# A decoder trunk on one core: four groups of modulation matmuls move to other places of the mixer, and two gate operations move behind a score update

## The chip, the cores and the metric

The kernel runs on one core of a Trainium2 chip. The metric is device time in microseconds (us), the median of three runs. The kernel before takes 1442.78 us (1442.36 to 1449.56). A profiled execution is taken beside the timed runs, and all durations below are from that one execution.

The core has a matrix engine (TensorE; PE in the rows, PEld for its weight loads), VectorE (DVE), ScalarE (ACT), GpSimd (POOL) and a queue engine (SP) that in this kernel issues the weight loads. Each engine works through its own list of instructions in order and waits on semaphores for the others.

## The reference

One step of a two-layer decoder trunk, for a prompt of 256 tokens and 8 single-token samples (264 columns together), with a model width of 1024, all in float32. A layer is: a SwiGLU block, a mixer, and a second SwiGLU block. Cut to what matters here:

```python
mod = (c @ w_ada[l] + b_ada[l]).reshape(B, N_SUB, 3, D_MODEL)   # adaLN: 9 blocks of 1024 columns a layer
h = ada_norm(x, norm_gain[l, 1], mod[:, 1, 0], mod[:, 1, 1])
y, ... = mixer_block(h, ...)          # branches A (HGRN2), B (RG-LRU), C (GLA), merged, times w_out
x = x + mod[:, 1, 2] * y

# branch B inside mixer_block
r, i = sigmoid(conv @ wa + ba), sigmoid(conv @ wx + bx)
log_a = -RG_C * r * softplus(-lam)
a, u  = exp(log_a), sqrt(-expm1(2 * log_a)) * i * conv
h_t   = a_t * h_(t-1) + u_t           # a scan over the tokens
y_b   = gelu(gb) * h
```

Branches A and C are gated linear recurrences. Inside a block of tokens the kernel forms their decayed scores in nine levels (pairs of tokens at distance 1, 2, 4, ... 128): at each level TensorE multiplies q and k, VectorE puts the result in the score tile and multiplies q, k and the decays for the next level.

## The kernel before

**Units.** The weights come as tiles of at most 128 x 1024 values (512 KB), called units here. Both layers have 436 units, 82 of them in each mixer. For a unit, SP loads a tile into one of six raw buffers; ScalarE rounds it to a high part (`whi`, line 450); VectorE subtracts to get the low part (`wlo`, line 458); and TensorE makes three matmuls for each 128 x 128 block (lines 493 to 495: high weight by high and by low activation, low weight by high activation), 24 in a full unit.

**Steps.** Every engine runs over the same list `MIX` of the mixer's 82 units, written out by hand. At step u, ScalarE and VectorE split unit u + 3 (`LOOK` is 3), then take the bank of unit u from TensorE, and then do whatever tables of numbers put at this step: `AT`, `EARLY_AT`, `HEAD_AT`, `PE_LV` for the score levels, `RG_AT` for branch B. The tables fix each engine's order at the time of writing; nothing is chosen at run time. In step u = `PE_LV` + 1, VectorE calls `keep` and `update` for a score level, and only after that come the entries of `RG_AT`. Unit numbers that matter below: 20 to 25 are branch B's gate weights and its `bg` columns, 26 to 29 are the values of branch C (`cv`), 30 to 33 and 34 to 37 the output gates of C (`cg`) and A (`ag`), and 38 to 45 the merge gate `ma`.

**The adaLN blocks.** `w_ada` is also read in tiles of 512 KB. Blocks 6 and 7 of a layer (the shift and scale of the second SwiGLU block) are computed inside the mixer, each in two groups of four tiles. The table `MIX_ADA` holds the units after which TensorE runs a group (line 679, 32 recorded matmuls); two steps after the second group of a block, VectorE turns the sums and adds the bias (lines 1730 and 1736), and after block 7 it also forms the norm's gains (line 1754).

**The raw buffers.** A group's four tiles use the same six raw buffers as the units. `load_order` puts them behind the load of unit place + 3. A load waits until the load six places earlier in the list has been used:

```python
            if c >= RAW:
                was, m = LOADS[c - RAW]
                if was == "m":
                    sp.wait_ge(lo_done, m + 1 + SLOTS)   # the unit's low part is made
                else:
                    sp.wait_ge(S["ada_used"], m + 1)     # TensorE has used the adaLN tile
```

So a group's last tile waits for the low part of unit place + 1, the next unit's load (place + 4) for that of place + 2, and the loads from place + 6 on for the group itself. SP issues in order, so a load that waits holds all behind it.

**Branch A's outer products.** At step 16 VectorE turns the samples' values (`vrA`); GpSimd writes them to memory (`v_rows`, line 1147) and reads them back spread over all partitions (`xA`, line 1161); ScalarE multiplies them at step 21.

**Branch B's gate.** `RG_AT` puts the two operations called `scaled` (lines 2207 and 2209: (r + 1) times the input, and the decay plus 1) at step 30, and the product `u` and the first half of the scan at step 32.

Of the kernel before, what the change touches and what calls it, by code (L numbers as in the profile page):

```python
# [48 lines left out]
    return l * UNITS + BASE[stage] + k  # L49


MIX_ADA = (10, 16, 29, 71)
ADA_BLOCKS = [(0, 1), (0, 0)]
ADA_FIRST = {}
RING = 8
# [3 lines left out]
def plan_ada():  # L59

    for l in range(NL):
        for f, places, blocks in (
                (0, (("in0", 16), ("in0", 28), ("in0", 41), ("out0", 11)), [(l, 2), (l, 3), (l, 4), (l, 5)]),
                (1, (("in1", 18), ("in1", 36), ("out1", 11)), [(l, 8), (l + 1, 0), (l + 1, 1)])):
            if f:
                for n, place in enumerate(MIX_ADA):
                    ADA_FIRST[(l, "mix", place)] = (8 * len(ADA_BLOCKS) + 4 * n, 4)
# [170 lines left out]


PE_LV = {'A': (17, 20, 24, 28, 31, 33, 38, 43, 45), 'C': (24, 28, 33, 38, 43, 45, 47, 50, 54)}  # L240
RG_AT = {'tanh': 22, 'gate': 25, 'exp': 26, 'square': 28, 'scaled': 30, 'root': 29, 'u': 32, 'scan': 32, 'y': 35, 'high': 37, 'low': 37}


BATCHES = [("A", 0), ("A", 1), ("A", 2), ("A", 3), ("C", 0), ("C", 1)]
# [2 lines left out]
def trunk(nc, x_prompt, x_sample, c_prompt, c_sample, state_hgrn, state_conv, state_rglru, state_gla,  # L247
# [4 lines left out]
    with ctx:  # L252
# [150 lines left out]
        def wait(eng, name, L, i=0):  # L403

            eng.wait_ge(S[name], L * PER[name] + i + 1)
# [95 lines left out]
        def evacuated(eng, L, what, j):  # L501

            group_done(eng, L, "mix", GI[(what, j)])
# [718 lines left out]
        def _(act):  # L1222
            def a(out, in_, func, **k):
                return nc.scalar.activation(out, in_, func, **k)  # L1224
# [28 lines left out]
            def A_(ins):  # L1253

                ins.then_inc(act_seq, 1)
                seq[0] += 1

            def own(L):
                act.wait_ge(act_seq, seq[0])
# [164 lines left out]
            def mixer(L):  # L1424
# [11 lines left out]
                for u, (kind, what, j) in enumerate(MIX):  # L1436
# [100 lines left out]
                    for t in range(2):  # L1537
                        if u == AT["C_vT"][t] + 1:
                            wait(act, "C_vT", L, t)
                            a(VT["C"][:, t], AUX[1][:, :], ACT.Copy).then_inc(S["C_vTe"], 1)  # L1540
                    if u == RG_AT["tanh"]:
                        evacuated(act, L, "wa", 3)
                        for jj in range(4):
                            c, c2_ = PC["nsp"] + jj, PC["nsp2"] + jj
                            A_(a(GT["A"][:, jj], tmp[:, 4 + jj], ACT.Tanh, scale=par_all[:, L, c:c + 1], bias=par_all[:, L, c:c + 1]))
                    if u == RG_AT["exp"]:
                        own(L)
# [4 lines left out]
                        last.then_inc(S["rg_tanh"], 1)  # L1552
                    if u == RG_AT["root"]:
                        wait(act, "rg_nt", L)
                        a(GT["A"][:, :], GT["A"][:, :], ACT.Sqrt).then_inc(S["rg_sqrt"], 1)
                    if u == RG_AT["high"]:
                        wait(act, "yb", L)
# [91 lines left out]
        def _(dve):  # L1649
# [12 lines left out]
            def V_(ins):  # L1662

                ins.then_inc(dve_seq, 1)
                seq[0] += 1
# [266 lines left out]
            def mixer(L):  # L1932
# [32 lines left out]
                def update(br, li):  # L1965

                    n_h = 4 if br == "A" else 2
                    q_, k_ = Q[br][:, :, 0:T], K[br][:, :, 0:T]
                    wait(dve, br + "_mm", L, li - 1)
                    if li == 1:  # L1970
                        if br == "A":
                            wait(dve, "A_f", L)
                        else:
                            wait(dve, "C_f", L)
                        tt(q_, q_, B[br][:, :, 0:T], ALU.mult).then_inc(S[br + "_up"], 1)
                        return
                    m = 2 ** (li - 2)
                    d = decay(br, m).rearrange("p h (n two o) -> p h n two o", two=2, o=1)
                    shape = [P, n_h, T // (2 * m), m]
                    qv, kv = halves(q_, m), halves(k_, m)  # L1980
                    if li < 9:
                        tt(qv[:, :, :, 1], qv[:, :, :, 1], bc(d[:, :, :, 0], shape), ALU.mult)
                    last = tt(kv[:, :, :, 0], kv[:, :, :, 0], bc(d[:, :, :, 1], shape), ALU.mult)
                    if li < 9:
                        dv = decay(br, m).rearrange("p h (n two) -> p h n two", two=2)
                        last = tt(decay(br, 2 * m), dv[:, :, :, 0], dv[:, :, :, 1], ALU.mult)
                    last.then_inc(S[br + "_up"], 1)
# [52 lines left out]
                for u, (kind, what, j) in enumerate(MIX):  # L2040
# [151 lines left out]
                    for br in "AC":  # L2192
                        for li in range(9):
                            if u == PE_LV[br][li] + 1:
                                keep(br, li)
                                update(br, li + 1)
                    if u == RG_AT["gate"]:
                        evacuated(dve, L, "wx", 3)
                        V_(v.scalar_tensor_tensor(bx, bx, 1.0, cv, ALU.add, ALU.mult))
                    if u == RG_AT["square"]:  # L2200
                        wait(dve, "rg_tanh", L)
# [141 lines left out]
```

## Time and profile before

| what | value |
|---|---|
| median of three runs | 1442.78 us |
| the profiled execution's own time | 1443.82 us |
| its span, first to last instruction | 1442.0 us |
| TensorE busy | 1421.0 us (99%) |
| VectorE busy | 940.0 us (65%) |
| ScalarE busy | 807.0 us (56%) |
| mean granted TensorE clock | 0.996 of full |
| DMA, mean over the span | 224 GB/s |

The table is read from the top: where one engine is busy nearly all the time, the others count only where they make it wait. The records of matmuls overlap (one lasts about 0.28 us, and the next starts 0.12 us after it), so short waits of TensorE have to be read from the distance of starts as well as from idle time. A mixer lasts some 287 us: the first from 246 to 533 us, the second from 948 to 1235 us.

### The profile page before, as it was taken

To read this page: it belongs to the slowest core of one execution; us is meant where nothing else is said; L and a number is where in the kernel's file an instruction comes from. 1 tells how busy PE (TensorE), PEld (TensorE's weight loads), DVE (VectorE), ACT (ScalarE), POOL (GpSimd) and SP (SyncE) were. 2 spreads that over 40 slices of the span, in tenths; PEclk is the share of its full clock that TensorE was granted. 3 is DMA by queue.
4 is the path that set the end of the run, shared out by engine and by line. 5 is a ranking of instruction groups with operands and counts; after the bars stand their busy time and mean duration, and the time that the engine had idled before them with its cause. 6 is when DMAs were issued, how large, how long until landed. Compare 5 with 4: busy or idle time off the path is not lost.

```text
span 1442.0 us, 32781 instructions
## 1 busy us (share of the span) xinstructions
PE 1421.0 (99%) x13780; PEld 1360.8 (94%) x13780; DVE 940.0 (65%) x1605; ACT 807.0 (56%) x1332; POOL 87.5 (6%) x131
## 2 busy tenths in 40 slices
PE   6999999999999999999999999999999999999998
PEld 4999999999999999999999999999999999999998
DVE  3665447788875697555586555577797677955553
ACT  2554435887666475444464434468876655644443
POOL 1040000001110120000000000000111002000000
PEclk9999999999999999999999999999999999999999
DMA  9988896698995679787768988776999657775661
GB/s 339 282 259 265 246 290 188 172 263 251 249 236 143 180 197 284 213 251 248 203 199 263 284 271 253 199 204 189 264 246 260 184 154 210 231 236 155 179 189 51
DMA packets 460036, 323.73 MB, mean 224 GB/s; under 512 B 11219, under 2 KB 435707, under 8 KB 459890
## 3 DMA queue, kind: packets, MB, share of 16 engines
q1 hardware_dynamic: 452240, 299.96, 71.1%
q0 software_dynamic: 6880, 20.41, 5.1%
q8 instruction: 109, 1.79, 0.5%
q10 hardware_dynamic: 770, 1.27, 0.2%
q14 instruction: 37, 0.30, 0.1%
HBM read 313.29 MB, written 8.37 MB: 223 GB/s over the span
## 4 chain that ended last, share of the span: by engine, by line
PE 88%; DVE 4%; issue 2%; ACT 2%; DMA 2%; SPq 1%; POOL 0%; DVEq 0%; ACTq 0%; POOLq 0%
PE bank L493 27%; PE bank L494 26%; PE bank L495 26%; PE bank L679 4%; SPq L551 1%; DVE wlo L458 1%; DMA first<-in_w_ada 1%; PE bank L846 1%; PE bank L874 1%; PE bank L893 1%; ACT whi L450 0%; ACT xA L1224 0%; DMA xA<-v_rows 0%; DMA v_rows<-vrA 0%; DVE x L1848 0%
## 5 line engine op out<-in xcount | busy, mean ns | idle before, releaser
L458 DVE TENSOR_TENSOR wlo<-raw,whi 128x1024 fp32r<-128x1024 f32 (+1 forms) x436 | 518.1, 1203 | 339.3 <-ACT whi L450 338.6
L493 PE MATMUL bank<-hH,whi 128*128 128x264 f32 x2048 | 587.1, 287 | 0.4 <-DVE wlo L458 0.4
L494 PE MATMUL bank<-hL,whi 128*128 128x264 f32 x2048 | 580.5, 283 | 0.0
L495 PE MATMUL bank<-hH,wlo 128*128 128x264 f32 x2048 | 580.0, 283 | 0.0
L450 ACT ACTIVATE whi<-raw 128x1024 fp32r<-128x1024 f32 (+1 forms) x436 | 442.2, 1033 | 185.6 <-PE bank L495 174.4
L493 PEld LDWEIGHTS bank<-hH,whi 128*128 128x128 f32 x2048 | 385.6, 188 | 13.9 <-issue 12.2
L494 PEld LDWEIGHTS bank<-hL,whi 128*128 128x128 f32 x2048 | 386.0, 188 | 0.0
L495 PEld LDWEIGHTS bank<-hH,wlo 128*128 128x128 f32 x2048 | 384.1, 188 | 0.0
L493 PE MATMUL bank<-hidH,whi 128*128 128x264 f32 x704 | 200.6, 285 | 0.0
L495 PE MATMUL bank<-hidH,wlo 128*128 128x264 f32 x704 | 200.1, 284 | 0.0
L494 PE MATMUL bank<-hidL,whi 128*128 128x264 f32 x704 | 199.5, 283 | 0.0
L1224 ACT ACTIVATE hidH<-hid 128x264 fp32r<-128x264 f32 x88 | 37.3, 424 | 173.0 <-DVE hid L1651 173.0
L493 PEld LDWEIGHTS bank<-hidH,whi 128*128 128x128 f32 x704 | 132.4, 188 | 1.3 <-issue 1.2
L495 PEld LDWEIGHTS bank<-hidH,wlo 128*128 128x128 f32 x704 | 132.7, 188 | 0.0
L494 PEld LDWEIGHTS bank<-hidL,whi 128*128 128x128 f32 x704 | 132.3, 188 | 0.0
L493 PE MATMUL bank<-uH,whi 128*128 128x274 f32 x320 | 94.5, 295 | 0.2
L494 PE MATMUL bank<-uL,whi 128*128 128x274 f32 x320 | 92.8, 290 | 0.0
L495 PE MATMUL bank<-uH,wlo 128*128 128x274 f32 x320 | 92.5, 289 | 0.0
L1224 ACT ACTIVATE sil<-bank 128x264 f32<-128x264 f32 x76 | 29.7, 391 | 98.5 <-PE bank L495 98.5
L493 PE MATMUL bank<-yH,whi 128*128 128x264 f32 x256 | 73.8, 288 | 0.0
L495 PE MATMUL bank<-yH,wlo 128*128 128x264 f32 x256 | 72.7, 284 | 0.0
L494 PE MATMUL bank<-yL,whi 128*128 128x264 f32 x256 | 72.6, 284 | 0.0
(330 smaller groups left out, 1659.1 us busy)
## 6 DMA issues: line engine op xcount, KB each, us to landing
raw<-in_w_ffn_in SPq DMA_DIRECT2D x176, 512.0 KB, 4.8
raw<-in_w_in SPq DMA_DIRECT2D x120, 512.0 KB, 5.6
ring<-in_w_ada SPq DMA_DIRECT2D x96, 512.0 KB, 6.6
raw<-in_w_ffn_out SPq DMA_DIRECT2D x64, 512.0 KB, 4.9
raw<-in_w_ada SPq DMA_DIRECT2D x32, 512.0 KB, 4.1
raw<-in_w_ffn_out SPq DMA_DIRECT2D x32, 384.0 KB, 4.7
first<-in_w_ada SPq DMA_DIRECT2D x16, 512.0 KB, 12.3
raw<-in_w_out SPq DMA_DIRECT2D x16, 512.0 KB, 5.3
```

Source lines behind the costliest of these rows:

```text
L450: nc.scalar.activation(whi[:, s, 0:w], raw[:, r, 0:w], ACT.Copy).then_inc(hi_done, 1)
L458: nc.vector.tensor_tensor(wlo[:, s, 0:w], raw[:, r, 0:w], whi[:, s, 0:w].bitcast(F), ALU.subtract).then_inc(lo_done, 1)
L493: nc.tensor.matmul(out, a, rh, start=start, stop=False)
L494: nc.tensor.matmul(out, a, rl, start=False, stop=False)
L495: return nc.tensor.matmul(out, b, rh, start=False, stop=stop)
L551: sp.dma_start(first[:, n], src).then_inc(first_in[FIRST_OF[n]], 16)
L679: last = mm(ps[32 * j:32 * j + 32, 0:256].rearrange("p (b i) -> p b i", i=32), cst[:, kt], src[:, j], start=(kt == 0), stop=(kt == KT - 1))
L846: last = mm(out, k_[:, r_], q_c, start=True, stop=True)
L874: mm(o, v0, sc[br][:, h, 0:T], start=True, stop=False)
L893: last = mm(AUX[base][0:dk, h * P:(h + 1) * P], KTT[br][:, t, h * dk:(h + 1) * dk], VT[br][:, t, h * P:(h + 1) * P], start=(t == 0), stop= ...
L1224: return nc.scalar.activation(out, in_, func, **k)
```

## The change

The groups stand after units 14, 28, 52 and 67 in place of 10, 16, 29 and 71, and `scaled` stands at step 32 in place of 30. No instruction is added or removed; both layers change alike.

```diff
-MIX_ADA = (10, 16, 29, 71)
+MIX_ADA = (14, 28, 52, 67)
-RG_AT = {'tanh': 22, 'gate': 25, 'exp': 26, 'square': 28, 'scaled': 30, 'root': 29, 'u': 32, 'scan': 32, 'y': 35, 'high': 37, 'low': 37}
+RG_AT = {'tanh': 22, 'gate': 25, 'exp': 26, 'square': 28, 'scaled': 32, 'root': 29, 'u': 32, 'scan': 32, 'y': 35, 'high': 37, 'low': 37}
```

The table moves instructions on TensorE, VectorE and SP; ScalarE and GpSimd keep their order. On VectorE at the end of step 30 (the vrC and gC rows are branch C's values and gate; the adaT and mod rows are the turn of adaLN block 6):

```order
 L2074 STREAM_TRANSPOSE vrC<-vC 128x32 x4
 L2137 SCALAR_TENSOR_TENSOR gC<-gC,bank 128x264
-L2207 SCALAR_TENSOR_TENSOR XB<-tmp,XB 128x1056
-L2209 TENSOR_SCALAR tmp<-tmp 128x1056
+L1730 STREAM_TRANSPOSE adaT<-bank 128x256
+L1651 TENSOR_TENSOR mod<-adaT,par_all 128x72
 L458 TENSOR_TENSOR wlo<-raw,whi 128x1024
 L2137 SCALAR_TENSOR_TENSOR gC<-gC,bank 128x264
```

The two `scaled` operations leave this step, and the turn of block 6, which stood in step 18, comes here. On VectorE in step 32, where the kA and xA rows are the end of the update of branch A's level, and the last two rows are `u` and the scan:

```order
 L1651 TENSOR_TENSOR kA<-kA,xA 128x4x16x8
 L1651 TENSOR_TENSOR xA<-xA 128x4x16
+L2207 SCALAR_TENSOR_TENSOR XB<-tmp,XB 128x1056
+L2209 TENSOR_SCALAR tmp<-tmp 128x1056
 L1651 TENSOR_TENSOR XB<-gA,XB 128x1056
 L2218 SCALAR_TENSOR_TENSOR tmp<-tmp,XB 128x256 x2
```

The two operations now stand behind the update and just ahead of `u`. On SP, the loads of the first mixer, from its first unit on; before:

```order
L431 DMA raw<-in_w_in 128x8x128 x14
L431 DMA raw<-in_w_ada 128x1024 x4
L431 DMA raw<-in_w_in 128x8x128 x6
L431 DMA raw<-in_w_ada 128x1024 x4
L431 DMA raw<-in_w_in 128x8x128
L431 DMA raw<-in_rg_wa 128x4x128
L431 DMA raw<-in_w_in 128x8x128 x3
L431 DMA raw<-in_rg_wx 128x4x128
L431 DMA raw<-in_w_in 128x8x128 x7
L431 DMA raw<-in_w_ada 128x1024 x4
```

And after:

```order
L431 DMA raw<-in_w_in 128x8x128 x18
L431 DMA raw<-in_w_ada 128x1024 x4
L431 DMA raw<-in_w_in 128x8x128 x3
L431 DMA raw<-in_rg_wa 128x4x128
L431 DMA raw<-in_w_in 128x8x128 x3
L431 DMA raw<-in_rg_wx 128x4x128
L431 DMA raw<-in_w_in 128x8x128 x6
L431 DMA raw<-in_w_ada 128x1024 x4
L431 DMA raw<-in_w_in 128x8x128 x16
```

Of the three groups whose tiles were loaded by unit 32, two are left; the second of them goes ahead of the load of unit 32 instead of behind it.

## Rows read from the trace of the kernel before

**Rows 1.** The page: span, and busy time of the engines.

```profile
span 1442.0 us, 32781 instructions
PE 1421.0 (99%) x13780; PEld 1360.8 (94%) x13780; DVE 940.0 (65%) x1605; ACT 807.0 (56%) x1332; POOL 87.5 (6%) x131
```

**Rows 2.** One stretch: length, busy PE, PEld, DVE, ACT, POOL, clock, DMA, GB/s.

```profile
39.20:1429.00 1389.80, 1388.10 (x13445) 1335.89 (x13444) 922.31 (x1562) 792.03 (x1300) 82.69 (x115) 1.00 0.77 223
```

**Rows 3.** Waits of TensorE: who for whom, total us, times, longest.

```profile
PE bank L846 <- DVE xA L1651: 0.7, 2, 0.5
```

**Rows 4.** Timeline of TensorE round the group at place 10: start, duration.

```profile
279.81 0.28 PE L494 MATMUL bank<-hL,whi 128*128 128x264 f32 x1
279.93 0.28 PE L495 MATMUL bank<-hH,wlo 128*128 128x264 f32 x1
280.15 1.93 PE L679 MATMUL bank<-raw,cst 128*32 128x256 f32 x32
282.01 0.39 PE L493 MATMUL bank<-hH,whi 128*128 128x264 f32 x1
282.24 0.29 PE L494 MATMUL bank<-hL,whi 128*128 128x264 f32 x1
```

**Rows 5.** Chain of waits: start, length; a group of eight tiles, one of four.

```profile
86.44 3.59 PE bank L679 x64
...
280.22 1.86 PE bank L679 x32
```

**Rows 6.** Timeline of TensorE: the small blocks at places 28, 52 and 67.

```profile
341.73 0.64 PE L915 MATMUL bank<-st,qs 128*32 128x256 f32 x8
...
429.93 0.65 PE L923 MATMUL bank<-xA,ones 128*32 128x264 f32 x8
...
483.81 0.71 PE L936 MATMUL bank<-xA,ident 32*128 32x264 f32 x4
```

**Rows 7.** Timeline of VectorE, steps 10 to 12; in brackets idle before and releaser.

```profile
286.44 0.48 DVE L2156 TENSOR_SCALAR bC<-bank,par_all 128x256 f32<-128x256 f32 x1 [2.33 <-PE bank L807]
...
292.32 1.22 DVE L458 TENSOR_TENSOR wlo<-raw,whi 128x1024 fp32r<-128x1024 f32 x1
```

**Rows 8.** SP's loads, issue to landing: from 265 to 276, then 275 to 292.

```profile
DMA to landing us min/median/max: 3.5/3.7/4.7
...
DMA to landing us min/median/max: 4.2/6.6/8.3
```

**Rows 9.** Timeline of ScalarE: high parts of units 32 and 33.

```profile
343.19 1.05 ACT L450 ACTIVATE whi<-raw 128x1024 fp32r<-128x1024 f32 x1
...
349.90 1.06 ACT L450 ACTIVATE whi<-raw 128x1024 fp32r<-128x1024 f32 x1 [1.61 <-DMA raw<-in_w_in]
```

**Rows 10.** Timeline of VectorE, steps 27 to 32.

```profile
341.83 2.45 DVE L458 TENSOR_TENSOR wlo<-raw,whi 128x1024 fp32r<-128x1024 f32 x2 [2.65 <-ACT whi L450]
...
346.11 1.22 DVE L458 TENSOR_TENSOR wlo<-raw,whi 128x1024 fp32r<-128x1024 f32 x1
...
353.90 1.24 DVE L2207 SCALAR_TENSOR_TENSOR XB<-tmp,XB 128x1056 f32<-128x1056 f32 x1
355.18 0.71 DVE L2209 TENSOR_SCALAR tmp<-tmp 128x1056 f32<-128x1056 f32 x1
...
360.62 0.22 DVE L1651 TENSOR_TENSOR xA<-xA 128x64 f32<-128x64 f32 x1
```

**Rows 11.** Timeline of VectorE, step 18: the turn of an adaLN block.

```profile
313.05 0.43 DVE L1730 STREAM_TRANSPOSE adaT<-bank 128x256 f32<-128x256 f32 x1
313.52 0.23 DVE L1651 TENSOR_TENSOR mod<-adaT,par_all 128x72 f32<-128x72 f32 x1
```

**Rows 12.** Timeline: unit 38's low part on VectorE, its first matmul on TensorE.

```profile
371.66 1.21 DVE L458 TENSOR_TENSOR wlo<-raw,whi 128x1024 fp32r<-128x1024 f32 x1
...
374.63 0.28 PE L493 MATMUL bank<-hH,whi 128*128 128x264 f32 x1
```

**Rows 13.** Timeline of ScalarE, second layer, step 21: the outer products.

```profile
1024.00 1.28 ACT L1224 ACTIVATE xA<-xA,kA 128x128 f32<-128x128 f32 x4 [2.48 <-DMA xA<-v_rows]
```

## The prediction

> **What bounds the kernel now.** I read the page first, then one long stretch, then TensorE's waits, and only then the other engines at the places where the change puts something. The page says TensorE is busy 99% of 1442.0 us [rows 1]. In the stretch from the first unit to the last it is idle 1389.80 - 1388.10 = 1.7 us [rows 2], and 0.7 us of that are two waits, one in each mixer, for VectorE's score update at step 32 [rows 3]. The clock there is 1.00, the full one. So there is little to win: the 1.7 us of idle time, and what TensorE loses at the change from one kind of matmul to another. There is more to lose, since VectorE, ScalarE and the loads run only a few units ahead in the first half of a mixer.
>
> What a group costs is read at place 10. From the last matmul before it to the second one behind it there are 282.24 - 279.93 = 2.31 us; two ordinary starts are 0.12 us each [rows 4], so the group adds 2.07. In the chain a group of eight tiles takes 3.59 us and one of four 1.86 [rows 5]: the second four add 1.73, and that is their matmuls alone. The other 0.34 us are the break, the way out of the 128*128 form of the units and back into it. With eight groups in two layers the breaks are 2.7 us; with the 1.7 us of idle time that is a ceiling of 4.4 us, or 0.3%, on any gain.
>
> **The change, part by part.** All terms are per layer.
>
> *Breaks.* Places 10, 16, 29 and 71 have the group between plain units. The new places 28, 52 and 67 already have a block of another form, so a break is shared [rows 6]. At 28 the block ends in 128*32 matmuls, the form of the group, and at 52 too: I take the whole 0.34 saved at each. At 67 the form is 32*128, so only the way out of the units is shared: 0.20, a bit over half. At 14 the block before the group has the units' own 128*128 form: 0.1. The trace of before has no such neighbours, so each lies between 0 and 0.34, and all four between 0 and 1.36; my sum is 0.98.
> The Trainium skill, TensorEngine Tiling (Array Packing), Key Properties, says that changing the tiling mode, not just the tile, drains the engine. By that sentence alone, 28 and 52 save all, and 14 and 67 nothing but what the order of forms leaves; the sum would be 0.68 to 0.98, inside my bounds.
>
> *Place 14, a tile that lands late.* The group's last tile needs the raw buffer of unit 15, freed by that unit's low part, which VectorE makes at 292.32 [rows 7]. Just before, VectorE waited 2.33 us for TensorE at 286.44 [rows 7]; with no group at 10 TensorE comes 2.07 earlier and nearly all of that wait goes, but the low part then waits a little for ScalarE, so it ends at about 291.8 and not at 293.5. The tile lands 3.5 to 4.7 us later [rows 8], at 295.3 to 296.5. TensorE, 2.07 us ahead, ends unit 14 and its transposes at about 293.8 and wants the fourth tile three quarters of the group later, at 295.1. A wait of 0.2 to 1.4; I take 0.35, from the low end, since no other load is then under way. Bounds 0 and 1.4.
>
> *Places 16 and 18.* The group and VectorE's turn go (2.07 and 0.7 us, [rows 4, 11]). TensorE enters units 17 to 27 some 1.8 us earlier. ScalarE waits for TensorE at steps 18 and 19, again at 26, and loads come without the catch-up burst, so it follows. The exception is step 21: there it waits for the spread values read back from memory, 2.48 us in the second layer [rows 13], and these hang on GpSimd's transfers, which no unit moves. With fewer loads in the queue I expect them earlier by about as much: 0 in the first layer, 0.3 in the second, bounds 0 and 2.07.
>
> *Place 28 instead of 29, and `scaled`.* This is the largest term. Now unit 32's load stands behind the four tiles. It waits for the buffer of unit 30, whose low part is the first of the two at 341.83 and ends at 343.05 [rows 10]. In a burst of six the first load lands after 4.2 us, the shortest of its row [rows 8]: at 347.25. Before, ScalarE made that high part at 343.19 [rows 9] from a tile long landed. Now it can't end before 348.3, all behind it on ScalarE waits too, and VectorE, free for the low part at 346.11 [rows 10], starts it 2.2 us later. On the way to the update, `scaled` is gone (1.24 + 0.71, with overlap 1.9 [rows 10]) and the turn is new (0.43 + 0.23, say 0.7 [rows 11]). So the update, which ended at 360.8 [rows 10], is 2.2 - 1.9 + 0.7 = 1.0 us later relative to TensorE's units, and TensorE, which already waited there [rows 3], restarts 1.0 later. The 0.34 saved at 28 vanishes in that wait. Unit 33's own high part waited 1.61 us for its load before [rows 9]; with unit 32 first, that wait goes, and is in the count. Below, the term is -0.8: the wait of 0.45 gone and the 0.34 kept. Above, with a landing of 6.6 us in place of 4.2 [rows 8], it is +3.4. I stay at the first-of-burst 4.2.
>
> *Behind the update.* `scaled` in step 32 makes VectorE 1.9 us later from there, 3 in all. Unit 38's low part ended at 371.66 + 1.21 = 372.87 and was wanted at 374.63 [rows 12]: a lead of 1.76. TensorE being 1.0 later, this falls short by some 0.2; in the second layer I add 0.25. Bounds 0 and 1.
>
> *Places 52 and 67.* Here the low parts are further ahead of TensorE than in the mixer's first half, and tiles and units land in time: 0. At the mixer's end the turn and the gains no longer stand ahead of the last low parts, where TensorE waits in snatches: -0.2, between 0 and -0.4.
>
> *Sum.* First layer: -0.64 (breaks at 14, 52, 67) + 0.35 + 1.0 + 0.2 - 0.2 = +0.7. Second: -0.64 + 0.35 + 1.0 + 0.45 + 0.3 - 0.2 = +1.3. Together +2.0 us. Against the profiled execution's own 1443.82 (its span and 1.8 us round it) that is 1445.8; that execution lies 1.0 above the median of the runs, 1442.78, so I forecast 1444.8 us.
>
> **The rivals.**
> *The cover holds.* Unit 32's tile comes soon enough, or VectorE has enough in hand once `scaled` is out of the way, and no new wait comes up. For it: the net shift of the update is a difference of terms near 2 us, and half a microsecond turns its sign. Against it: the load can't be issued before 343.05. It gives -1.96 (breaks) - 0.7 - 0.4 = -3.1: 1439.7 us.
> *The transfers of step 21 stay where they are.* If GpSimd's write and read back take as long as before, ScalarE gains nothing from the missing group, TensorE runs into it at units 25 and 26, and the 2.07 us come back as a wait while they are still paid at 52. For it: the 2.48 us of [rows 13]. Against it: the burst of loads that now lies beside these transfers goes. It decides from about half of 2.07 on. Both layers: 1444.8 - 0.3 + 4.1 = 1448.6 us.
> *Unit 32's load lands late.* The slower side. At 8.3 us, the longest of [rows 8], in place of 4.2 the update is 4.1 later in each layer: 1444.8 + 8.2 = 1453.0 us. Against it: it is the first of its burst, and of a burst of six the first was the quickest [rows 8]. It decides against "no change" from a landing of some 6.8 us on.
> The Trainium skill, DMA: Bandwidth & Descriptors, Issuing engines are not separate DMA queues, says that transfers issued by SP and GpSimd run on the same engines and interleave. By it GpSimd's state transfers could slow this load, and SP's burst the transfers of step 21; the last two rivals are its two sides, and no row of before settles which.
>
> **How the numbers follow.** The forecast 0.47, the cover holds 0.30, step 21 0.15, the late load 0.08. A measurement of this kernel can tell about 0.5%, 7.2 us, from no change. Faster by more is above the ceiling of 4.4 us and keeps 0.02 for what I misread. Slower by more needs most of the last rival or several upper bounds: 0.06. Same: 0.92. The forecast's own range is 1441.5 to 1448. The range that should hold 8 in 10 takes in the first rival to its bound (-2.7 - 0.9 - 0.6 = -4.2, 1438.6) and the second: 1438.6 to 1449.5.
>
> **What would show it.** In the profile after: TensorE's wait for the update (L846 on xA) grows from 0.7 to near 3 us in all; ScalarE waits about 3 us for a weight load at the high part of unit 32 and none at 33; the groups at 28 and 52 follow the small block 0.2 us after its last start, without the slow restart of the units between; TensorE waits some tenths for the fourth adaLN tile at 14. If the wait at step 32 is gone, the first rival is right. If matmuls of units 25 and 26 have gaps near 2 us, the second. If the sum moves over 7 us, my reading of what is in hand in the middle of the mixer is wrong.

## The result and the profile after

The changed kernel takes 1452.36 us (median of 9 runs, 1449.58 to 1453.19) against 1443.05 us for the kernel before (9 runs): a ratio of 1.0056, 95% interval 1.0045 to 1.0067. It is slower by 9.3 us. The forecast was 1444.8, and the time lies outside the range that was given. The profiled execution took 1453.19 us with a span of 1451.4, that is 9.4 us more than the profiled execution of before.

The page of the kernel after, to be held against [rows 1], and its packets of instructions (queue, packets, MB, share of 16 DMA engines):

```profile
span 1451.4 us, 32781 instructions
PE 1422.7 (98%) x13780; PEld 1364.5 (94%) x13780; DVE 941.8 (65%) x1605; ACT 806.3 (56%) x1332; POOL 86.9 (6%) x131
...
q8 instruction: 109, 1.79, 0.5%
```

TensorE has the same 13780 matmuls and is busy only 1.7 us longer; the rest is idle time. Its waits from 45 to 1440 us (whom it waited for; us in total, times, longest), where [rows 3] was the only one of note before:

```profile
PE bank L495 <- issue: 2.8, 1, 2.8
PE bank L494 <- issue: 2.1, 1, 2.1
PE bank L846 <- DVE xA L1651: 1.8, 2, 1.6
PE bank L679 <- DMA raw<-in_w_ada: 1.0, 1, 1.0
PE bank L915 <- issue: 0.9, 1, 0.9
```

The two longest, and the last, are called "issue": TensorE waited for nothing that the profile shows. To see where the time is lost, I took the start of each unit's first matmul in both traces; the table has the jumps of the difference (after minus before, us), worked out from these starts.

| where | first layer | second layer |
|---|---|---|
| group at 10 gone | -1.96 | -1.96 |
| group at 14 | +2.31 | +3.25 |
| group at 16 gone | -1.96 | -1.96 |
| group at 28 | +3.20 | +1.73 |
| group at 29 gone | -1.98 | -2.13 |
| wait for the update, before unit 34 | -0.45 | +1.29 |
| inside units 34 and 35 | +3.92 | +4.65 |
| groups at 52 and 67 | +1.73, +1.86 | +1.73, +1.86 |
| group at 71 gone | -1.95 | -1.95 |
| small steps | -0.37 | -0.52 |
| sum | +4.35 | +5.99 |

Together 10.3 us; 1.0 us was won ahead of the first mixer, where the change moves nothing (in the seven kernels whose lists begin alike the first unit starts anywhere from 34.6 to 36.5 us), and the rest is the loss. Behind a group that is gone the unit's second matmul comes another 0.11 us earlier; that stands in the small steps, so an old group costs 2.07 us and not 1.96. The row that nobody had forecast is "inside units 34 and 35". The timeline of TensorE there, first layer (start, duration, engine, line, count, idle before it and releaser):

```profile
359.00 0.74 PE L846 MATMUL bank<-qA,kA 128*32 128x16 f32 x64 [0.26 <-DVE xA L1651]
359.66 0.73 PE L846 MATMUL bank<-qC,kC 64*32 64x16 f32 x64
360.32 0.39 PE L493 MATMUL bank<-hH,whi 128*128 128x264 f32 x1
...
363.68 0.37 PE L493 MATMUL bank<-hH,whi 128*128 128x264 f32 x1
366.16 0.39 PE L494 MATMUL bank<-hL,whi 128*128 128x264 f32 x1 [2.11 <-issue]
```

and second layer:

```profile
1069.30 0.28 PE L494 MATMUL bank<-hL,whi 128*128 128x264 f32 x1
1072.40 0.40 PE L495 MATMUL bank<-hH,wlo 128*128 128x264 f32 x1 [2.82 <-issue]
```

The first layer's +3.20 at the group at 28 holds the "issue" gap of 0.9 us at 339 us; the second layer, without such a gap there, has +1.73. The two long gaps lie between two of the three matmuls of one weight block, where no semaphore stands. What else happens then is seen in the DMA queues. First from 363.6 to 364.8 us (queue, packets, MB, share of 16 engines), then from 1069.8 to 1071.0:

```profile
q0 software_dynamic: 46, 0.19, 72.1%
q8 instruction: 1, 0.02, 5.7%
q1 hardware_dynamic: 4, 0.00, 1.1%
```

```profile
q1 hardware_dynamic: 229, 0.11, 31.7%
q0 software_dynamic: 9, 0.03, 22.4%
q8 instruction: 1, 0.02, 5.5%
```

A packet of instructions lands in each of the two, and TensorE goes on 1.4 us later. These 109 packets are TensorE's own list: its 13780 matmuls and 13780 weight loads make 253 to a packet. I numbered TensorE's records in order of start, those of its sequencer too. The first one behind each "issue" gap of this kernel (339.16, 363.68, 1069.30 us) has number 6593, 7362 and 21186: 193, 194 and 194 past a multiple of 256. So the list comes in pieces of 256, and at these three places the next piece was not there. The score level just ahead explains the hurry: its 128 small matmuls and their 128 loads, as many as a piece has, pass in 360.32 - 359.00 = 1.3 us. The kernel before shows the same on a small scale: in the second half of this level its record 7361, 193 past a multiple of 256, starts 0.24 us after the one ahead of it, where 0.01 is usual, and the half takes 0.99 us in place of 0.73:

```profile
361.56 0.99 PE L846 MATMUL bank<-qC,kC 64*32 64x16 f32 x64
```

The Trainium skill, Runtime: NRT & Kernel Launch, Instruction fetch mechanics, says that instructions come in blocks of 256 while the block before is executed, and that this is mostly hidden because instructions are dispatched more slowly than blocks arrive. The 253 a packet agree with the first half; the 1.3 us and the gaps speak against the second, and the measurement decides.

The gaps are not all of the cost. The granted clock (the last figure but two) in stretches ahead of and behind them; columns are the stretch, its length, busy PE, PEld, DVE, ACT and POOL, clock, DMA share, GB/s:

```profile
360.30:363.70 3.40, 3.40 (x39) 3.38 (x29) 3.33 (x5) 0.47 (x2) 0.90 (x1) 1.00 0.87 282
366.20:369.40 3.20, 3.20 (x18) 3.20 (x19) 3.19 (x7) 0.00 (x0) 0.00 (x0) 0.65 0.79 192
1067.30:1069.30 2.00, 2.00 (x21) 2.00 (x17) 1.93 (x3) 0.00 (x0) 0.07 (x1) 1.00 0.99 332
1072.40:1075.80 3.40, 3.40 (x20) 3.40 (x21) 3.37 (x9) 2.23 (x6) 0.00 (x0) 0.69 0.80 214
```

Behind each of these two gaps the clock falls from the full 2.4 GHz to the lower level of 1.2 GHz for a while, matmuls start every 0.22 us in place of 0.12, and unit 36 is another 1.54 us late. The three stalls (at 339, 364 and 1069 us) are 1.15 + 2.36 + 2.98 = 6.5 us over an ordinary distance of starts, the slow clock 2 x 1.54 = 3.1: together 9.6, the size of the whole loss.

### The profile page after: what moved, and what is told of

The parts are those of the page before. It is cut to its first block, busy times and chain, and to the rows that moved or that the text cites. A ratio compares the mean times of both kernels' runs of the same rounds, so it can differ in the third digit from the quotient of the medians.

```text
span 1451.4 us, 32781 instructions
## 1 busy us (share of the span) xinstructions
PE 1422.7 (98%) x13780; PEld 1364.5 (94%) x13780; DVE 941.8 (65%) x1605; ACT 806.3 (56%) x1332; POOL 86.9 (6%) x131
## 4 chain that ended last, share of the span: by engine, by line
PE 89%; DVE 3%; ACT 2%; issue 2%; DMA 2%; SPq 1%; DVEq 0%; ACTq 0%
PE bank L493 27%; PE bank L494 26%; PE bank L495 26%; PE bank L679 4%; SPq L551 1%; DVE wlo L458 1%; PE bank L846 1%; DMA raw<-in_w_ffn_in 1%; DMA raw<-in_w_ada 1%; PE bank L874 1%; ACT whi L450 1%; PE bank L893 1%; DVE x L1848 0%; PE bank L915 0%; ACT tmp L1224 0%
## 5 line engine op out<-in xcount | busy, mean ns | idle before, releaser
L493 PEld LDWEIGHTS bank<-hH,whi 128*128 128x128 f32 x2048 | 387.6, 189 | 13.4 <-issue 11.6
```

The costliest lines, as they stand in the source:

```text
L493: nc.tensor.matmul(out, a, rh, start=start, stop=False)
```

## The experiments

Ratios are to runs of the kernel before on the same chip. "Stall" is an "issue" gap less an ordinary distance of starts.

**Shift the pieces, leave the mixers alone.** Moving a group moves TensorE's list too: from unit 30 to 52 the changed kernel has two groups behind it where before had three, 64 instructions fewer. Narrow matmuls at the start put them back.

```diff
-            for bank in AUX:
-                for c in range(0, 512, T):
-                    mm(bank[:, c:c + T], ones[:, 0:P], ones[:, :], start=True, stop=True)
+            for i in range(8 + 16):
+                c, w = (i // 4 * T, T) if i < 8 else (0, 8)
+                mm(AUX[i % 4][:, c:c + w], ones[:, 0:P], ones[:, 0:w], start=True, stop=True)
```

> The changed kernel with 16 more narrow matmuls of ones behind the eight at its start: each is two weight loads and two matmuls in the records, so TensorE's list has 64 instructions more ahead of everything else, and nothing in the mixers moves. Theory (instruction fetch): TensorE's list comes in pieces of 256 instructions, one packet each on the queue of kind instruction, and the three gaps of the changed kernel at 339.16, 363.68 and 1069.30 us (1.15, 2.36 and 2.98 us over an ordinary pitch, 6.5 in all) stand where a piece was not there yet. 64 more instructions put the piece boundaries at units 30 to 52 back to where they lie in the kernel before: no gap above 1 us inside units 28 to 36 in either layer, and 1452.4 - 6.5 + 0 to 2 for the pad = 1446 to 1448 us. Rival (the bursts of loads, or what VectorE does at steps 28 to 36, hold TensorE up by themselves): the gaps stay where they are, 1452 to 1454 us.

1448.52 us, ratio 1.0036 (1.0020 to 1.0052), span 1446.5. No "issue" gap is left in the mixers; the wait that the prediction had foretold comes out instead:

```profile
PE bank L846 <- DVE xA L1651: 3.3, 2, 1.7
PE bank L493 <- DVE gA L2137: 0.8, 1, 0.8
```

By starts it is 1.77 and 1.85 us (0.61 and 0.45 before). Behind the first the clock fell to 0.59 and cost 1.54 us; behind the second it stayed at 1.00:

```profile
360.80:364.30 3.50, 3.50 (x63) 3.47 (x47) 3.40 (x6) 0.00 (x0) 0.42 (x1) 0.59 0.93 301
1064.80:1068.30 3.50, 3.49 (x85) 3.42 (x61) 3.40 (x6) 0.00 (x0) 0.00 (x0) 1.00 0.93 303
```

The 1.54 us are more than the half microsecond by which the time lies above what I expected. Without its stalls the change still costs 5.3 us (1448.52 against 1443.21): of the 9.3 us only some 4 go with the pad, since the waits that the stalls had hidden come out.

The reverse, on the kernel before: `range(8 + 48)`, 192 instructions, the changed kernel's boundaries modulo 256.

> The kernel before with 48 more narrow matmuls of ones at its start, 192 instructions: modulo 256 this puts the piece boundaries at units 30 to 52 where the changed kernel has them, with places and gate operations as before. Theory (instruction fetch): gaps of 1 to 3 us appear inside units 28 to 36 of one layer or both, without a visible wait, and the time is 1443 + 1 to 4 for the pad + 1 to 6 = 1445 to 1453 us. Rival: no gap above 1 us in those units, 1444 to 1447 us from the pad alone.

1461.39 us, ratio 1.0113 (1.0081 to 1.0144). This is above what I expected: in the profiled execution (1459.46 us) the first unit starts 10.3 us later than before. But the gaps appear, at the end of unit 34 in the first layer and inside it in the second (behind the matmuls at 376.03 and 1077.77 us):

```profile
PE bank L494 <- issue: 2.3, 1, 2.3
...
PE bank L493 <- issue: 1.4, 1, 1.4
```

With `range(8 + 24)` the stalls should move to other steps:

> The kernel before with 24 more narrow matmuls of ones at its start, 96 instructions. From the starts in the trace of before, TensorE would then go through a piece and what it holds ahead in 2.3 us at 1029, 3.1 us at 328 and 4.8 us at 1043 us of that profile, and in 7 us or more at 359 and 1063. Theory (instruction fetch): the stalls stand elsewhere than in the changed kernel, at steps 24 to 28 (one or two of 1.5 to 4 us in the second layer, one of 1 to 3 us in the first), and none at units 34 to 36: 1443 + 1 to 3 for the pad + 3 to 9 = 1447 to 1455 us. Rival (the gaps belong to the work of units 34 to 36, whatever the boundaries): no gap above 1 us at steps 24 to 28, 1444 to 1446 us.

1449.23 us, ratio 1.0037 (1.0021 to 1.0052). The two stalls stand at 331.82 and 1033.65 us, in units 26 and 25, 1.4 and 1.2 us; none at units 34 to 36, and none at 1043, where I had allowed one. They are 2.6 of the 3.3 us that the profiled execution (1447.09 us) takes more than that of before; what else is in the median was not traced. First layer:

```profile
331.82 0.35 PE L493 MATMUL bank<-hH,whi 128*128 128x264 f32 x1
333.33 0.39 PE L494 MATMUL bank<-hL,whi 128*128 128x264 f32 x1 [1.15 <-issue]
```

And with `range(8 + 8)`:

> The kernel before with 8 more narrow matmuls of ones at its start, 32 instructions; by the starts in the trace of before no piece is then gone through in less than 5.5 us. Theory (instruction fetch): no stall anywhere behind the start, 1443 + 0 to 1 for the pad = 1443 to 1444.5 us. Rival (any shift of the boundaries costs, or the pad itself holds up the start by as much as in the longer pads): 1446 us or more.

1443.8 us, ratio 0.9997 (0.9986 to 1.0008), no stall. Where the boundaries lie decides, not that something was added.

**The two halves of the change.** `'scaled': 32` alone on the kernel before:

> The kernel before with only the two gate operations moved from step 30 to step 32. TensorE's list is that of before, so no gap from a late piece. Theory: the wait for the update behind unit 32 (0.7 us in two) goes, unit 38's low part comes some tenths late: 1442 to 1444 us. Rival (the two operations behind the update are what holds TensorE up in units 34 to 36): 1447 us or more, with gaps there.

1444.55 us, ratio 1.0000 (0.9985 to 1.0016). The waits for the update go (0.09 us left in each), but TensorE, quicker there, now runs into one late piece that I had not expected:

```profile
PE bank L846 <- issue: 0.9, 1, 0.9
```

`MIX_ADA = (14, 28, 52, 67)` alone:

> The changed kernel with the gate operations back at step 30: only the four groups are moved. Theory (instruction fetch): the boundaries are those of the changed kernel, so the gaps in units 28 to 36 stay, and the wait for the update behind unit 32 comes on top where it does not cover them: 1450 to 1456 us. Rival (the gate operations made the loss): 1441 to 1446 us, no gaps.

1452.6 us, ratio 1.0061 (1.0046 to 1.0076). Waits for the update of 2.16 and 3.81 us, stalls of 1.21 and 1.13. So `scaled` behind the update does save some 2 us of wait at the update, but TensorE only comes sooner to the missing piece: what one wait gives back, the other takes.

**Is it the group at 28?** `MIX_ADA = (10, 16, 52, 67)`, `scaled` at 30:

> The kernel before with the third and fourth group moved to 52 and 67; the groups at 10 and 16 and the gate operations stay. From unit 30 to 52 TensorE's list then holds one group, 64 instructions, less than before, so the boundaries of its pieces of 256 lie there as in the changed kernel. Theory (instruction fetch): gaps of 1 to 3 us without a visible wait inside units 28 to 36 of at least one layer, although no group and no burst of loads stands between units 23 and 48: 1443 - 0.7 (shared breaks, 0.23 and 0.10 in each layer) + 3 to 9 (stalls and the slow clock behind them) = 1445 to 1451 us. Rival (the group at 28 with its loads, or the one at 14, makes the gaps): none above 0.8 us, 1441 to 1443 us.

1451.76 us, ratio 1.0052 (1.0039 to 1.0065). The stalls come at the same two records (7362 and 21186), but at 0.6 us each they are smaller than expected. The loss is mainly another:

```profile
PE bank L846 <- DVE xA L1651: 5.0, 2, 2.5
```

Counted from the mixer's first matmul the update ends at 116.9 us in the first layer, as before (116.9), while TensorE is there at 114.2 in place of 116.2. The group at 29 was TensorE's work while VectorE made the update; without it the same 2 us are waited, and the clock falls with both waits (0.64 and 0.50 in the 3.3 us behind them), 1.54 us in the first layer.

**What delays a packet.** Two of GpSimd's transfers, which fill the DMA engines from 358 to 362 us, cut to an eighth in the changed kernel:

```diff
-                g.dma_start(dst, st[:, i % 2]).then_inc(st_out[i % 2], 16)
+                g.dma_start(dst[:, 0:1 if i == 1 else NB], st[:, i % 2, 0:1 if i == 1 else NB]).then_inc(st_out[i % 2], 16)
...
-                    g.dma_start(vb[rows_], vd[L, "AC".index(br), h:h + 1].rearrange("o b v -> o (b v)").broadcast_to([n, NB * P])).then_inc(vb_in, 16)
+                    g.dma_start(vb[rows_, 0:nb * P], vd[L, "AC".index(br), h:h + 1, 0:nb].rearrange("o b v -> o (b v)").broadcast_to([n, nb * P])).then_inc(vb_in, 16)
```

(`nb` is 1 for batch 2 and 8 otherwise.)

> The changed kernel with two of GpSimd's transfers cut to an eighth, the second store of branch A's sample states and the spread of the values for the next batch, so that seven eighths of these states are not written and of these values not refreshed. In the changed kernel both run from 358 to 362 us, when the packet of instructions is 4.5 us late, and again 700 us later. Theory (the packet of instructions waits in the DMA engines behind other transfers, GpSimd's above all): it starts 2 us or more earlier there, the stalls at 363.7 and 1069.3 us shrink from 2.4 and 3.0 us to under 1 us, and with the slow clock behind them 4 to 8 us go: 1444 to 1448 us. Rival (a fixed time from the boundary to the packet): the stalls stay, 1450 to 1453 us.

1447.64 us, ratio 1.0018 (1.0005 to 1.0031). The stall at 363.7 is gone, the one at 1069.3 falls from 3.0 to 1.0 us, with no slow clock behind; the two packets start at 361.05 and 1064.15 us. Counted from the 160th record past a multiple of 256 (see the last section), they start 1.5 and 1.9 us late in place of 4.5 and 3.9. The stall at step 28 (339 us), where no GpSimd transfer runs, stays: 1.5.

**The prediction's largest term by itself.** `MIX_ADA = (14, 29, 52, 67)` with `scaled` at 32 and the pad of 64, so that unit 32's load is ahead of the group's tiles:

> The changed kernel with 64 more instructions at TensorE's start, and the second group after unit 29 in place of 28, so that its four tiles stand behind the load of unit 32 and not ahead of it. Theory of the prediction (unit 32's late load makes the score update late): counted from the mixer's first matmul the update ends 1 to 2 us before the 116.0 and 116.3 us of the kernel with the group at 28 and this pad, TensorE waits under 0.6 us for it in each layer in place of 1.8, and no slow clock follows: 1444 to 1446 us. Rival (the chain on ScalarE and VectorE up to the update is the bound, and TensorE waits only because it has one group less behind it at unit 33): the update stays at 115.7 to 116.4 us, the waits at 1.3 to 1.9, 1447 to 1449 us.

1444.73 us, ratio 1.0005 (0.9993 to 1.0017). The update ends at 114.5 and 114.3 us, 1.5 and 2.0 earlier than with the group at 28; TensorE waits 0.09 us in each layer. ScalarE makes unit 32's high part without a wait, where with the group at 28 and this pad it waits 3.69 us for the load and starts at 345.15:

```profile
341.74 1.05 ACT L450 ACTIVATE whi<-raw 128x1024 fp32r<-128x1024 f32 x1
```

One stall of 0.9 is left:

```profile
PE bank L846 <- issue: 0.9, 1, 0.9
PE bank L493 <- DVE gA L2137: 0.6, 1, 0.6
```

The rival falls: the late load made the wait.

**Place 14 by itself.** `MIX_ADA = (14, 16, 29, 71)`:

> The kernel before with the first group after unit 14 in place of 10, and nothing else. Theory of the prediction (the group's fourth tile is freed and lands late there): TensorE waits 0.2 to 0.6 us inside the group in each layer and the time is 1443.3 + 0.5 to 1.2 = 1443.8 to 1444.5 us, or less where the waits behind it take it up. Rival (the tile lands in time): no wait, 1443 us.

1448.67 us, ratio 1.0030 (1.0014 to 1.0046), well above what I expected. By the second matmul behind it the group at 14 costs 2.25 and 2.32 us, 0.2 to 0.3 more than at 10 (2.07), as foretold. The surprise is the group at 16, whose tiles now stand two units behind the other four in the same six buffers. Timeline of TensorE, first layer:

```profile
302.10 1.31 PE L679 MATMUL bank<-raw,cst 128*32 128x256 f32 x16
304.04 0.64 PE L679 MATMUL bank<-raw,cst 128*32 128x256 f32 x8 [0.63 <-DMA raw<-in_w_ada]
305.40 0.64 PE L679 MATMUL bank<-raw,cst 128*32 128x256 f32 x8 [0.73 <-DMA raw<-in_w_ada]
```

That is 2 us in each layer, 4.0 in the profiled execution (1447.8 us), and it does not arise in the change, which moves that group to 28.

**Versions.** `MIX_ADA = (10, 16, 29, 52)`, `scaled` at 30, pad `range(8 + 8)`:

> The kernel before with only the last group moved, from 71 to 52, where it shares a break (0.23 us in each layer by the profile of the changed kernel), and 32 more instructions at TensorE's start, the distance at which no piece is gone through in under 5 us. By the theory of instruction fetch and of the group at 29 as TensorE's work while VectorE makes the update: no stall, waits for the update of 0.4 to 0.6 us as before, 1443.3 - 0.5 + 0 to 0.5 = 1442.8 to 1443.3 us. Rival (the loads of the group at 52 collide with the units there): a wait of 0.5 us or more between units 50 and 58, 1444 us or more.

1442.47 us (12 runs), ratio 0.9983 (0.9971 to 0.9995): below both kernels, by a small amount that is clear of the interval. How much of it the group at 52 made is not shown: of the 1.4 us in the profiles 0.7 lie ahead of the first mixer, and the shared break gives 0.33 us in each layer (the 0.23 is its part at the first matmul behind the group). No stall, no new wait above 0.2 us:

```profile
PE bank L846 <- DVE xA L1651: 0.8, 2, 0.4
PE bank L1078 <- issue: 0.5, 1, 0.5
PE bank L493 <- ACT tmp L1224: 0.2, 1, 0.2
```

`MIX_ADA = (10, 29, 52, 67)`, `scaled` at 32, pad `range(8 + 22)`:

> A version made of what the runs so far showed: groups at 10, 29, 52 and 67 (none at 14, where the fourth tile is late, and none ahead of unit 32's load), the gate operations behind the update as in the change, and 88 more instructions at TensorE's start, which puts the piece boundaries 24 instructions from those of before at steps 17 to 52. Theory: no stall above 0.5 us behind the start, waits for the update under 0.3 us, one wait of some 0.8 us in the second layer for unit 38's low part, and two shared breaks in each layer: from the 1444.7 us with the second group at 29 and the first at 14, less 0.4 and 0.3 for place 14 and 0.9 for its one stall, 1442.5 to 1443.5 us. Rival (without the group at 16, TensorE is 2 us ahead at unit 33 and waits for the update): waits of 1 to 2 us there, with the slow clock behind them 1445 us or more.

1444.91 us, ratio 1.0008 (0.9996 to 1.0021), above what I expected. The waits for the update are 0.09, as the theory has it, but the start came 1.6 us later, VectorE holds unit 38 up by 0.75 us in both layers, and at 1080.48 us a piece is late by 0.65.

## Why the prediction was wrong

The step that failed is the accounting of a moved group in *The change, part by part*: it was priced by its matmuls, its breaks and its loads. Its 64 places in TensorE's own list were not in it. They decide where the pieces of 256 begin, and from unit 30 to 52 the new places put a beginning just inside the score levels at steps 28 and 33 (13 and 59 records into them in the first layer). Missing term: 6.5 us of stalls. A second omission made it dearer: each wait was priced at its length, and 3.1 us came from the clock behind two of them. Of the 9.4 us the forecast had 2.0; with both terms it would have been 11.6. The surplus is the 1.0 us won at the start and the first layer's wait for the update, which the stall at 339 us took up (-0.45 in place of +1.0); the other misses nearly cancel. What was forecast was too small as well: with the pad, and so without stalls, the change costs 5.3 us.

Point by point:

- *What bounds the kernel.* Right: the whole loss is idle or slow time of TensorE. The closing sentence of the prediction did not hold: it puts a sum that moves over 7 us down to a wrong reading of what is in hand in the middle of the mixer, but that reading came within 0.4 us (*Place 28*, below), and what carried the sum over 7 us were the stalls, which stand in none of its rows.
- *Breaks.* Right, in size too: by the second matmul behind it a group costs 2.07 at the old places, 1.73 at 28 (second layer) and 52 and 1.86 at 67, so 0.34, 0.34 and 0.21 are shared, where I had 0.34, 0.34 and 0.20. At 52 the unit behind starts slowly in both kernels (the second matmul 0.22 us after the first), with the group ahead of it or the small block alone. The first two lines are from before, the others from after:

```profile
430.52 0.39 PE L493 MATMUL bank<-hH,whi 128*128 128x264 f32 x1
430.74 0.28 PE L494 MATMUL bank<-hL,whi 128*128 128x264 f32 x1
...
432.17 1.91 PE L679 MATMUL bank<-raw,cst 128*32 128x256 f32 x32
434.01 0.39 PE L493 MATMUL bank<-hH,whi 128*128 128x264 f32 x1
434.24 0.28 PE L494 MATMUL bank<-hL,whi 128*128 128x264 f32 x1
```

- *Place 14.* Right: 0.26 us more than an old group in the first layer, where I had 0.25 (0.35 less the 0.1 of the break). In the second 1.2, near the upper bound: the tile lands late by the 1.0 in the waits above.
- *Places 16 and 18.* Right: against the mixer's start, unit 17 begins 1.7 us earlier in the first layer (1.8 foretold) and 0.7 in the second, where the tile at 14 took the rest. TensorE has no gap at units 25 and 26, so the rival on step 21's transfers is out, and the 0.3 us of the second layer with it.
- *Place 28 and `scaled`.* The mechanism is shown, on ScalarE in the kernel after, to be held against [rows 9]:

```profile
344.29 1.06 ACT L450 ACTIVATE whi<-raw 128x1024 fp32r<-128x1024 f32 x1 [3.81 <-DMA raw<-in_w_in]
```

  Without stalls it makes the wait 1.2 and 1.4 us longer, where I had 1.0; with the load ahead of the tiles it vanishes.
- *Behind the update.* 0 in the kernel after, where the stalls may have given VectorE time (not shown); 0 and 0.98 with the pad, forecast 0.2 and 0.45.
- *Places 52 and 67, the mixer's end.* No waits, as forecast; behind the group at 71 the difference of the starts stays within 0.05 us, so the end gives nothing in place of 0.2.
- *The late load as a rival* had 1453.0, next to the time measured, by luck: its mechanism did not occur, since unit 32's load landed 4.0 us after its issue, as in the forecast.

What the runs don't settle is why the clock stayed full behind one wait of 1.85 us and fell behind one of 1.77.

## What to carry to other kernels

A moved block of instructions also shifts the boundaries of the pieces in which an engine's list arrives; where hundreds of short instructions run within a few microseconds, count where the boundary falls, and look for gaps marked "issue" between instructions that have no semaphore between them. A small pad at the start tells such a stall from a cause in the kernel's own order, since it changes no order behind it; it can shift the start itself, so run a pad of another length beside it. Filler work that stands just ahead of a wait can be worth its full length (2 us for the group at 29), and a wait can cost more than its length.

## What the hardware showed that was not expected

- In nine of the fourteen profiles TensorE has 16 "issue" gaps of 0.3 us or more inside the mixers. The first record behind each is 193 or 194 past a multiple of 256, and starts 1.2 to 1.6 us after a packet of instructions has landed. The other five profiles have none there.
- A packet takes 1.1 us, but it starts later the more traffic there is; only the run with GpSimd's transfers cut tests this, the rest is seen side by side. Counted from the 160th record past a multiple of 256, near the earliest point at which one was seen to start, with the traffic averaged from there to the start, and over five profiles (before, after, the pad of 64 and the two halves): with under 4 of the 16 DMA engines busy the median is 0.1 us (some 80 packets), with over 18 transfers under way at a time 2.5 (some 77), and with GpSimd's queue holding more than three engines 3.5, at most 8.1 (some 67).
- With waits of 2.16 us or more in the mixers TensorE's granted clock fell in all seven cases, in two of them shortly before the wait had ended. One of these two is the second layer of the kernel with places 10, 16, 52 and 67, where it is at the lower level for the whole stretch behind the wait:

```profile
1067.30:1070.60 3.30, 3.30 (x83) 3.24 (x76) 3.27 (x6) 0.00 (x0) 0.90 (x1) 0.50 1.16 336
```
